# Small products of a gated linear recurrence regrouped over the quarters of the array, and a row normalisation taken in halves

## What is computed

```
for l in range(DEPTH):
    h = _rmsnorm(x, norm_g[l])
    p = h @ w_in[l]                       # 8,904 columns, split among mixers A, B, C, D and gates
    ...
    od = _rwkv7(dr, dk, dv, ...)          # mixer D: per row, 4 heads of 64
    ...
    y = sum over branches of sigmoid(gate) * (branch @ w_branch)
    x = x + y @ w_out[l]
return _rmsnorm(x, final_g)

def step(state, xs):                      # mixer D
    sa = einsum('bhvk,bhk->bhv', state, -kkt)
    state = state * wt + sa (x) (kkt * at) + vt (x) kt
    return state, einsum('bhvk,bhk->bhv', state, rt)
```

## Time and profile before

| what | value |
|---|---|
| median of 3 runs | 2801.29 us (2797.76 to 2802.34) |
| the profiled execution | 2800.43 us |
| its span, first to last instruction | 2798.6 us |
| mean granted PE clock | 0.997 |
| busy: PE, VectorE, ScalarE, GpSimd | 98%, 57%, 35%, 29% of the span |

### The profile page before, as it was taken

How to read it: one execution, slowest core, us unless ns; L and a number is a source line. 1 busy time by engine, 2 the same in 40 slices (tenths; PEclk the granted TensorE clock), 3 DMA queues, 4 the chain that set the end, 5 groups by cost and what they waited for, 6 DMA issues and landing times.

```text
span 2798.6 us, 45940 instructions
## 1 busy us (share of the span) xinstructions
PE 2741.4 (98%) x18624; PEld 1491.4 (53%) x18624; DVE 1596.7 (57%) x2995; ACT 968.0 (35%) x1838; POOL 797.7 (29%) x582
## 2 busy tenths in 40 slices
PE   7999999999999999999999999999999999999998
PEld 4446444466574566544444464544765745655443
DVE  4689876744507742265237997667444078222743
ACT  3455665311224324500124556643112242344001
POOL 3333312411334332133032333124113342321420
PEclk9999999999999999999999999999999999999999
DMA  4221111201111123083042121112111111231721
GB/s 160 65 60 54 42 46 42 86 26 33 52 35 46 62 84 108 20 280 117 38 124 53 46 61 50 39 38 83 33 33 50 46 49 48 80 106 73 247 94 60
DMA packets 134218, 200.88 MB, mean 72 GB/s; under 512 B 7128, under 2 KB 89208, under 8 KB 133240
## 3 DMA queue, kind: packets, MB, share of 16 engines
q1 hardware_dynamic: 115416, 163.85, 18.6%
q10 hardware_dynamic: 18592, 34.09, 3.3%
HBM read 146.53 MB, written 44.59 MB: 68 GB/s over the span
## 4 chain that ended last, share of the span: by engine, by line
PE 44%; DVE 4%; ACT 1%; issue 1%; POOL 0%; ACTq 0%; DVEq 0%
PE ps L491 23%; PE ps L488 4%; PE ps L751 4%; PE ps L765 3%; PE ps L1086 1%; PE ps L1097 1%; PE ps L1950 1%; PE ps L1432 1%; PE ps L1110 1%; DVE arena L1830 1%; DVE arena L1572 1%; PE ps L2012 1%; PE ps L1942 0%; DVE arena L1556 0%; PE ps L1896 0%
## 5 line engine op out<-in xcount | busy, mean ns | idle before, releaser
L491 PE MATMUL ps<-hT,wr 128*128 128x512 f32 x1856 | 859.0, 600 | 3.4 <-PEq L2468 2.9
L491 PEld LDWEIGHTS ps<-hT,wr 128*128 128x128 f32 x1856 | 337.7, 191 | 372.3 <-issue 361.0
L491 PE MATMUL ps<-sums,wr 128*128 128x512 f32 x928 | 437.0, 599 | 2.4 <-issue 1.5
L667 POOL TENSOR_TENSOR gts<-gts,wr 128x512 f32<-128x512 f32 x96 | 156.7, 1632 | 630.1 <-ACT wr L542 421.7
L1186 DVE CUSTOM_DVE_ANT_0 arena<-ps,arena 128x640 f32<-128x640 f32 (+7 forms) x128 | 90.3, 705 | 337.6 <-PE ps L1086 322.8
L491 PEld LDWEIGHTS ps<-sums,wr 128*128 128x128 f32 x928 | 168.1, 190 | 190.0 <-issue 181.4
L542 ACT ACTIVATE wr<-ps 128x512 f32<-128x512 f32 x174 | 103.2, 593 | 382.4 <-PE ps L491 335.0
L751 PE MATMUL ps<-xo,arena 128*128 128x512 f32 x512 | 220.1, 592 | 0.0
L491 PE MATMUL ps<-wr 128*128 128x512 f32 x464 | 217.1, 599 | 0.0
L638 POOL TENSOR_TENSOR wr<-wr 128x512 f32<-128x512 f32 x57 | 82.6, 1449 | 392.9 <-PE ps L491 367.9
L1572 DVE TENSOR_SCALAR_CACHE_REDUCE arena<-arena,sm 128x384 f32<-128x384 uint16 (+7 forms) x256 | 192.8, 808 | 2.2
(11 more groups left out here) (310 smaller groups left out, 4263.4 us busy)
## 6 DMA issues: line engine op xcount, KB each, us to landing
wr<-in_w_in SPq DMA_DIRECT2D x62, 1024.0 KB, 5.3
gate_tanh<-gts ACTq DMA_DIRECT2D x128, 256.0 KB, 2.1
arena<-gate_tanh SPq DMA_DIRECT2D x128, 256.0 KB, 3.0
wr<-in_w_in SPq DMA_DIRECT2D x16, 512.0 KB, 3.8
arena<-in_w_branch SPq DMA_DIRECT2D x8, 1024.0 KB, 8.8
wr<-in_w_out SPq DMA_DIRECT2D x8, 1024.0 KB, 7.4
arena<-arena SPq DMA_DIRECT2D x36, 128.0 KB, 2.4
arena<-in_x SPq DMA_DIRECT2D x8, 512.0 KB, 7.2
```

The lines of the kernel that those rows point to most:

```text
L491: ins = pe.matmul(ap, lhsT=right(u, w_side)[:, kt, :], rhs=left(h_side, kt), start=fresh and kt == 0, stop=kt == half_k - 1, skip_group_ch ...
L667: pool.tensor_tensor(dst, dst, stage_of(u), ALU.add).then_inc(sg("pool_added"), 1)
```

## The change

The edits are of two kinds: D's instruction order, and the ends and starts of the layers.

In D: the values of a chunk are no longer a group of their own; `first_level` issues them in turn with level 1's Y of the same pair, into the bank S2 of that pair. `last_level` issues level 5's X of pair p in turn with level 5's Y of pair p+1, behind one fill and ahead of another. `added_values` goes kind by kind over two heads and two chunks. The transposes of v (L1924) use four banks in place of two. ScalarE's copies of the chunk values move behind both pairs.

Around it: rows are squared in halves of 512 columns, each as soon as its half is added (`half_rows`), and `normed` takes one row tile from mean to scaled row before the next is begun. PE turns pairs 0, 1 and 2 behind the second product of i = 1, 2 and 3, and only pair 3 behind the last product, in four banks. VectorE's six sums of `h` (`dve_h_sums`) are made by halves. GpSimd's fourth sum ahead of the barrier moves behind it. Ahead of C's search ScalarE takes fills up to mark 18 in place of 16.

```diff
-                if i == 2:
-                    return [(bk, (2 * n, 2 * n + 1)) for n, bk in enumerate((T, O, G[0], G[1]))]
+                if i == NT // 2 - 1:
+                    return [(bk, (2 * n, 2 * n + 1)) for n, bk in enumerate((T, O, S2[0], S2[1]))]
...
-                dve.tensor_tensor(s3, a11, a21, ALU.subtract).then_inc(sg("h_sums"), 1)
...
+                for n in range(2):
+                    kts = slice(half_k // 2 * n, half_k // 2 * (n + 1))
+                    dve.tensor_tensor(s3[:, kts], a11[:, kts], a21[:, kts], ALU.subtract).then_inc(sg("h_sums"), 1)
+                    dve.wait_ge(sg("h_sums"), 3 * n + 1)
+                    dve.tensor_tensor(a21[:, kts], a21[:, kts], a22[:, kts], ALU.add).then_inc(sg("h_sums"), 1)
+                    dve.wait_ge(sg("h_sums"), 3 * n + 2)
                     dve.tensor_tensor(s2[:, kts], a21[:, kts], a11[:, kts], ALU.subtract).then_inc(sg("h_sums"), 1)
...
-                pool.wait_ge(sg("next_w_sums"), 2)
-                pool.tensor_tensor(t4, b21, t2, ALU.subtract).then_inc(sg("next_w_sums"), 1)
...
-                        for turned in {2: (0,), 3: (1, 2, 3)}.get(i, ()):
-                            pe_turn_next(pe, turned)
+                        if l + 1 < DEPTH and p == 1 and i:
+                            pe_turn_next(pe, i - 1)
+                if l + 1 < DEPTH:
+                    pe_turn_next(pe, NT // 2 - 1)
...
+                    act.activation(H(16, 0.5), xin[:, row, 512 * n:512 * n + 512], ACT.Square, accum_out=total)\
+                       .then_inc(sg("squares_next"), 1)
...
+                def normed(r, half_first):
...
+                    dve.tensor_scalar(ssa[:, c], ssa[:, c], 1.0 / D, EPS, ALU.mult, ALU.add).then_inc(sg("half_mean"), 1)
...
+                    dve.scalar_tensor_tensor(msq[:, c], ssq[:, c], 1.0 / D, ssa[:, c], ALU.mult, ALU.add).then_inc(sg("mean_square_next"), 1)
...
+                    dve.reciprocal(inv[:, c], root[:, c]).then_inc(sg("inverse_next"), 1)
...
+                    normed(2 * i, 4 * i + 1)
+                    add(i, 6, i + 4, 0)
+                    jobs.stored(dve, ("out", i, 6))
+                    dve.engine_nop().then_inc(sg("new_rows"), 1)
+                    normed(2 * i + 1, 4 * i + 2)
...
-                    act_fills(act, ("beside search", 16))
+                    act_fills(act, ("beside search", 18))
...
-                    if l == 0:
-                        pool_w_sums(pool, 0, (1, 2, 3, 4))
+                    pool_w_sums(pool, 0, (4,) if l else (1, 2, 3, 4))
...
-                        ap = jobs.open(pe, ("vn", i), [T, O][i % 2])
+                        ap = jobs.open(pe, ("vn", i), [T, O, S2[0], S2[1]][i % 4])
...
+                    def first_level(p):
+
+                        e, key = p % 2, ("Y", p, 1)
+                        pe.wait_ge(sg(f"x_ready{e}"), 6 * (p // 2) + 1)
+                        y = jobs.open(pe, key, (T, O)[e])
+                        cv = jobs.open(pe, ("CV", p), S2[e])
                         for j, i in tiles(p):
+                            values = vn[:, i, :].rearrange("p (h v) -> p h v", h=4)
+                            for h in range(4):
+                                y0, v0 = 256 * j + CH * h, 256 * j + HD * h
+                                for c in range(2):
+                                    rows, to = half_rows(c, True), half_rows(c, False)
+                                    ins_y = pe.matmul(y[to, y0:y0 + CH], lhsT=at_[e][rows, j, h, :], rhs=xx[e][rows, j, h, :], start=True, stop=True)
+                                for c in range(2):
+                                    rows = half_rows(c, False)
+                                    ins_v = pe.matmul(cv[rows, v0:v0 + HD], lhsT=ct_[e][rows, j, h, :], rhs=values[rows, h, :], start=True, stop=True)
...
+                    def last_level(p):
...
+                                for c in range(2):
+                                    rows, to = half_rows(c, True), half_rows(c, False)
+                                    ins_y = pe.matmul(y[to, y0:y0 + CH], lhsT=at_[1 - e][rows, j, h, :], rhs=xx[1 - e][rows, j, h, :],
+                                                      start=True, stop=True)
+                                for c in range(2):
+                                    rows = half_rows(c, False)
+                                    ins_x = pe.matmul(x[rows, x0:x0 + CH], lhsT=yy[e][rows, j, h, :], rhs=xt[e][rows, j, h, :], start=True, stop=True)
...
+                            for m in range(2):
+                                for kind in range(3):
+                                    for h in (2 * m, 2 * m + 1):
+                                        for c in range(2):
+                                            e0, rows, c0 = HD * (h % 2), half_rows(c, False), 512 * c + 256 * j + HD * m
...
-                        chunk_values(p)
...
-                        chunk_values(p + 1)
-                        for lv in range(1, 6):
+                        for lv in range(1, 5):
                             for e in range(2):
-                                level_y(p + e, lv)
+                                if lv == 1:
+                                    first_level(p + e)
+                                else:
+                                    level_y(p + e, lv)
...
+                        level_y(p, 5)
+                        pe_fill(pe, D_FILL["Y"])
+                        last_level(p)
+                        pe_fill(pe, D_FILL["X"])
+                        level_x(p + 1, 5)
```

More of the change, by code:

```diff
@@ L958, in act_norm @@
                     if i:
[L959 to L965 removed]
+                        act.wait_ge(sg("mean_square_first"), i)
@@ L967, in dve_norm, with dve_norm_first @@
+                        act.activation(root[:, i - 1:i], msq[:, i - 1:i], ACT.Sqrt).then_inc(sg("root_first"), 1)
+            def dve_norm_first(dve):
                 for i in range(NT + 2):
-                    if i < NT and rows_step is not None:
-                        rows_step(i)
                     if 1 <= i <= NT:
                         c = slice(i - 1, i)
-                        dve.wait_ge(sg("squares_" + when), i)
-                        dve.tensor_scalar(msq[:, c], ssq[:, c], 1.0 / D, EPS, ALU.mult, ALU.add).then_inc(sg("mean_square_" + when), 1)
+                        dve.wait_ge(sg("squares_first"), i)
+                        dve.tensor_scalar(msq[:, c], ssq[:, c], 1.0 / D, EPS, ALU.mult, ALU.add).then_inc(sg("mean_square_first"), 1)
@@ L987, in dve_norm @@
-                    if when == "next" and l + 1 < DEPTH and i in (5, NT + 1):
-                        dve.wait_ge(sg("next_par_loaded"), 16)
-                        evac_next(dve, 1, (0,) if i == 5 else (1, 2, 3))
+                        dve.wait_ge(sg("root_first"), i - 1)
+                        dve.reciprocal(inv[:, c], root[:, c]).then_inc(sg("inverse_first"), 1)
+                        dve.wait_ge(sg("inverse_first"), i - 1)
+                        dve.tensor_scalar(xo[:, i - 2, :], xin[:, i - 2, :], inv[:, c], None, ALU.mult).then_inc(sg("rows_normed"), 1)
@@ new lines, in act_norm_next, with square @@
+            def act_norm_next(act):
+                squared = [0]
+                def square(row, n, total):
+                    if squared[0]:
+                        act.wait_ge(sg("squares_next"), squared[0])
+                    squared[0] += 1
+                    act.activation(H(16, 0.5), xin[:, row, 512 * n:512 * n + 512], ACT.Square, accum_out=total)\
+                       .then_inc(sg("squares_next"), 1)
+                for i in range(NT // 2):
+                    act.wait_ge(sg("half_rows"), 2 * i + 1)
+                    square(i, 0, ssa[:, 2 * i:2 * i + 1])
+                    if i and l + 1 < DEPTH:
+                        act.wait_ge(sg("next_par_loaded"), 16)
+                        evac_next(act, 0, i - 1)
+                    act.wait_ge(sg("half_rows"), 2 * i + 2)
+                    square(i + 4, 1, ssa[:, 2 * i + 1:2 * i + 2])
+                    for n in range(2):
+                        c = slice(2 * i + n, 2 * i + n + 1)
+                        act.wait_ge(sg("new_rows"), 2 * i + n + 1)
+                        square(i + 4 * n, 1 - n, ssq[:, c])
+                        act.wait_ge(sg("mean_square_next"), 2 * i + n + 1)
+                        act.activation(root[:, c], msq[:, c], ACT.Sqrt).then_inc(sg("root_next"), 1)
+                if l + 1 < DEPTH:
+                    evac_next(act, 0, NT // 2 - 1)
@@ new lines, in dve_out @@
+                for i in range(NT // 2):
+                    add(i, 0, i, 0)
+                    add(i, 1, i, 0, 0)
+                    jobs.stored(dve, ("out", i, 1))
+                    dve.engine_nop().then_inc(sg("half_rows"), 1)
+                    add(i, 2, i, 1)
+                    if i and l + 1 < DEPTH:
+                        dve.wait_ge(sg("next_par_loaded"), 16)
+                        evac_next(dve, 1, i - 1)
```

(19 more changed lines are left out.)

154 lines of the change are left out of this document (63 added, 91 removed).

## The result

The changed kernel takes 2784.12 us (median of 5 runs, 2780.94 to 2787.27) against 2800.78 of the kernel before (5 runs). The ratio is 0.9946, 95% interval 0.9935 to 0.9958: 15.1 us faster by the ratio, where 24.3 were forecast.

A forecast was written before the change was run, and what follows sets the result against it. PE, busy 98% of the span, was the bound. Packing 22.6, transposes 0.8, boundary -1.2, end 1.6 make 23.8 us off 2800.43: 2776.6, given as 2777.0 for the median; own range 2770 to 2784, 8 in 10 2769 to 2787.

The forecast's parts named there:

- rival 1: In D: dense groups outrun PE's instruction queue, two more waits a group, 9.2 us less gained, 2786; chance 0.13.
- Packing (a, b, c): In mixer D: (a) chunk values with level 1 8.4 us, (b) level 5 3.3, (c) added values 10.9; 22.6 together.
- Cover by VectorE and ScalarE: In D's levels 1 and 5: PE's waits for these engines priced at nothing, at worst 0.5 us a couple in level 5.
- rival 2: In D: the new orders do not pack and stay at 30 ns a record; 22.6 us go, 2799.6; chance 0.03.
- rival 3: In D's levels 1 and 5: PE waits for VectorE and ScalarE, giving back the gains there, 2788.7; chance 0.04.
- rival 4: In D's new groups: quarters get in each other's way, 64 ns a record, 74 us more, 2851; chance 0.02.
- Supply: In D: PE's waits for its own instructions stay at 8.1 us in sum, bounds 8 less and 8 more.
- Transposes of v: In D: four banks let PE run ahead of ScalarE, saving 0.4 us a layer, 0.8 in all.
- The halves of `dve_h_sums`: VectorE's sums of h made by halves: no gain, since the product with `s2` needs them all and their work is unchanged.
- Boundary, -1.2: Between layers: two turns add 3.5 us to PE's stream, GpSimd ends last at 8.4, 11.9 against 10.52; 1.2 lost.
- One slow stretch of clock at the restart I leave as it is: At layer 1's restart: the slow clock stays as before; one stretch more or less is 1.65 us.
- End of the program: At the last row's scaling on VectorE: half a square and no waiting behind the row before save 1.6 us, bounds 1.0 to 2.0.

The follow-up runs named there:

- again: The changed kernel with no edit, run a second time: median 2785.85 us, ratio 0.9948 to the kernel before; its profiled run took 2788.81.

## Why the prediction was right, and where it was off

The direction held, and the range, 2769 to 2787, holds the time; the likeliest value, 2777.0, is 7.1 us too low. Both medians, 2784.1 and 2785.9, lie at and beyond the upper edge of the forecast's own range, 2770 to 2784, and nearest to rival 1's 2786, which had 0.13: the wider range was right by the room that it gave to that rival. Of the 7.1, 4.3 are the terms below, read in the profile of the fastest run; the rest is that this run lies 3.2 below the median, where the forecast allowed 0.4. (Its own sum, with its 0.9, would give 2777.5.)

- **Packing (a, b, c).** Right: 22.6 forecast, 22.9 found in PE's own stream, at 15.9 ns for the first level, 17.0 to 18.1 with its edges for the last and 14.6 for the added values; by these paces alone the three terms come to some 22.8. The Trainium skill, "TensorE: Matmul & The Clock Gate", section "Wait — 56ns, not 53.3ns?", gives a floor of about 25 ns from start to start; it does not hold for these products, which alternate over the quarters.
- **Cover by VectorE and ScalarE.** Right: no such wait in the levels. With that and the paces, rivals 2, 3 and 4 are out.
- **Supply, "I put the sum of such waits at the same 8.1 us: nothing".** This is the step that failed, though its bounds held: 11.7 and 14.5 in two profiles, 3.6 to 6.4 us. What it left out: behind 20 of the 23 waits of 2 us or more in D the clock went slow for 3.4 us, some 1.65 us lost each time, and behind none of the shorter waits for a packet; that is once in the profile before, twice and three times in the two after. Rival 1 names the right cause, but its picture, two more short waits for each dense group, is not what came. The waits stand where the count of 256 puts them, and the long ones are those whose packet stands behind a weight load, a case that the earlier trace rows already showed and that I did not carry into the sum.
- **Transposes of v.** Forecast 0.8, measured 0.4. **The halves of `dve_h_sums`**, at nothing: PE waits 2.02 us in layer 0, 1.70 before, 0.3 lost.
- **Boundary, -1.2.** Mis-sized: 2.4 lost in the boundary stretch. In *again* it is 3.3, beyond the 3 that the prediction called wrong. The two turns cost 3.5 as said; the way behind the last product became 1.1 shorter, not 2.3. I had GpSimd last; VectorE is, since GpSimd's sums stretch its scaling by 0.94 and the turn runs at the slow clock (2.80 us against 1.91). "One slow stretch of clock at the restart I leave as it is" failed too: it is 6.8 to 13.7 us long with the new standstill.
- **End of the program.** 1.6 forecast, 1.6 measured.

For the profiled run the terms close: 22.9 - 2.8 (idle of both layers, v and sums in it) - 2.4 + 1.6 + 0.2 (clock in the layers) = 19.5, and 2800.43 - 2780.94 = 19.5. They close by their making, since 22.9 is what is left of the layers without idle and clock; the paces' 22.8 is the independent figure. By my own test, D shorter by under 17 us would be wrong: the layers are 20.4 shorter in one profile and 13.3 in the other, so the test itself depends on the run.

## What to carry to other kernels

When dense small products are packed tighter, count the instructions in them: where 256 pass faster than their packet comes, part of the time saved turns into waits a multiple of 256 apart, whatever product stands there. Look first for bulk loads that run during such stretches; moving two loads a layer into a stage with slower products brought some 6 us here (2778.4 against 2784.1). An engine that is left with one long standstill in place of several short ones may pay for it afterwards in clock.

## What was not expected of the hardware

- A load of 1 MB can keep an instruction packet from starting until it is nearly through: 34 of the 125 waits in D had their packet behind one, and PE stood 0.4 to 3.2 us, 2.0 or more in 23 of them. Behind no load it stood 1.8 at most. That a load delays a packet was seen in the earlier trace rows; that it is so regular was not expected.
- The slow clock at the boundary lasted 6.8, 10.2 or 13.7 us after one and the same standstill of 4.3 us, and its sum differs between runs of one program: 13.7 and 23.9 us in two profiles of the changed kernel. The slow clock and the waits, there and in D, set the two profiles of one program 7.9 us apart.
